# Convolution taps, channel statistics and the third branch's strips of a hybrid decoder layer in another order

## What is computed

```python
h = rms_norm(x) @ w_in                      # pool | u | v | a | g | gates 3*1024
p, u, v, ca, cg, gl = jnp.split(h, ...)
ya = pool_branch(p)                         # trailing-window means minus token, 4 linear maps
yb = u * (tril(W_s) @ layer_norm(v) + b)    # chunks of 128
y  = depthwise_conv31(ca * sigmoid(cg)) + conv_b
yc = silu(layer_norm(y))                    # mean and variance over 512 channels
ga, gb, gc = jnp.split(jax.nn.sigmoid(gl), 3, axis=-1)
merged = ga * (ya @ wb_pool) + gb * (yb @ wb_sgu) + gc * (yc @ wb_conv)
x = x + merged @ w_out
x = x + moe(rms_norm(x))                    # top 2 of 32 experts, 6.3 MB of weights each
```

## Time and profile before

| what | value |
|---|---|
| median of 3 runs | 1028.43 us (1027.98 to 1028.86) |
| the profiled execution | 1027.61 us, of which 1025.8 us are the span on the page |
| TensorE busy | 849.6 us (83%) |
| VectorE busy | 349.4 us (34%) |
| ScalarE busy | 199.2 us (19%) |
| mean granted clock of TensorE | 0.947 |
| bytes moved | 262.18 MB |

### The profile page before, as it was taken

How to read it: one execution, slowest core, us unless ns; L and a number is a source line. 1 busy time by engine, 2 the same in 40 slices (tenths; PEclk the granted TensorE clock), 3 DMA queues, 4 the chain that set the end, 5 groups by cost and what they waited for, 6 DMA issues and landing times.

```text
span 1025.8 us, 12405 instructions
## 1 busy us (share of the span) xinstructions
PE 849.6 (83%) x5199; PEld 582.1 (57%) x5199; DVE 349.4 (34%) x502; ACT 199.2 (19%) x304; POOL 89.3 (9%) x78
## 2 busy tenths in 40 slices
PE   1999999999999997996388898888878788787740
PEld 0899999999999997994133333323333223232310
DVE  3224856778777648125500000000000000000008
ACT  3421333222222353023011100100000001100003
POOL 2100000000000000000101111101101101011004
PEclk9999999999999998998599999999999989999995
DMA  9322222113133119737079999999999999999934
GB/s 276 107 83 83 83 83 81 42 50 128 62 107 121 42 54 357 292 124 292 17 282 420 420 420 419 419 418 420 419 418 420 421 419 421 420 419 419 412 137 194
DMA packets 73031, 262.18 MB, mean 256 GB/s; under 512 B 8359, under 2 KB 42307, under 8 KB 47840
## 3 DMA queue, kind: packets, MB, share of 16 engines
q1 hardware_dynamic: 67856, 252.46, 62.4%
q0 software_dynamic: 5120, 8.93, 2.4%
HBM read 256.09 MB, written 13.74 MB: 263 GB/s over the span
## 4 chain that ended last, share of the span: by engine, by line
PE 77%; DVE 11%; issue 6%; ACT 4%; DMA 2%; DVEq 0%; POOLq 0%; SPq 0%; ACTq 0%
PE ps L629 25%; PE ps L799 23%; PE ps L820 12%; PE ps L652 8%; PE ps L789 2%; PE ps L810 2%; DVE area L1438 2%; ACT area L1034 1%; DVE area L1113 1%; DVE xrows L1080 1%; ACT w_high L854 1%; DVE w_low L1100 1%; PE ps L600 1%; PE ps L714 1%; DVE xrows L1461 1%
## 5 line engine op out<-in xcount | busy, mean ns | idle before, releaser
L799 PE MATMUL ps<-area 128*64 128x512 f32 x1024 | 236.2, 615 | 29.8 <-issue 29.0
L799 PEld LDWEIGHTS ps<-area 128*64 128x64 f32 x1024 | 82.1, 141 | 181.5 <-issue 180.2
L629 PE MATMUL ps<-x_high,w_high 128*128 128x272 f32 x640 | 174.2, 290 | 0.6 <-DVE y_low L1258 0.6
L629 PE MATMUL ps<-x_low,w_high 128*128 128x272 f32 x640 | 173.3, 290 | 0.0
L1429 DVE TENSOR_TENSOR area<-ps,norm_cols 128x512 f32<-128x512 f32 x32 | 22.1, 692 | 432.3 <-PE ps L789 432.3
L820 PE MATMUL ps<-area 128*64 128x512 f32 x512 | 126.9, 641 | 14.8 <-ACT area L1034 14.8
L629 PE MATMUL ps<-x_high,w_low 128*128 128x272 f32 x640 | 133.1, 289 | 0.0
L629 PEld LDWEIGHTS ps<-x_high,w_high 128*128 128x128 f32 x640 | 121.1, 189 | 1.2 <-DVE w_low L1100 1.0
L629 PEld LDWEIGHTS ps<-x_low,w_high 128*128 128x128 f32 x640 | 121.2, 189 | 0.1
L1100 DVE TENSOR_TENSOR w_low<-area,w_high 128x2048 fp32r<-128x2048 f32 (+1 forms) x36 | 69.7, 1936 | 109.5 <-ACT w_high L854 109.5
L629 PEld LDWEIGHTS ps<-x_high,w_low 128*128 128x128 f32 x640 | 100.6, 189 | 0.0
(11 more groups left out here) (229 smaller groups left out, 860.1 us busy)
## 6 DMA issues: line engine op xcount, KB each, us to landing
area<-in_w_gate_e SPq DMA_DIRECT2D x32, 2048.0 KB, 32.4
area<-in_w_up_e SPq DMA_DIRECT2D x32, 2048.0 KB, 34.1
area<-in_w_down_e SPq DMA_DIRECT2D x32, 2048.0 KB, 34.4
area<-in_w_in SPq DMA_DIRECT2D x22, 1024.0 KB, 5.1
area<-in_w_out SPq DMA_DIRECT2D x4, 1024.0 KB, 10.5
area<-expert_rows SPq DMA_DIRECT2D x4, 1024.0 KB, 9.7
xrows<-in_x_prompt SPq DMA_DIRECT2D x4, 512.0 KB, 4.9
area<-in_w_branch_pool SPq DMA_DIRECT2D x4, 512.0 KB, 3.3
```

Of the source, the lines that this page charges most:

```text
L629: last = pe.matmul(ps[:, 2 * r + half, 0:HT], w[:, k, c * P:(c + 1) * P], src[:, k, half * HT:(half + 1) * HT], start=(k == 0 and len(part ...
L799: last = pe.matmul(ps[g * CAP:(g + 1) * CAP, 2 + s].rearrange("p (m f) -> p m f", m=2), xgT[s][:, k % 4, (k // 4) * CAP:(k // 4 + 1) * CAP ...
```

## The change

Four things are done. (1) The 124 taps are dealt out anew: the counts between VectorE's other steps differ, among them 8 in place of 4 between the variance of v and its reciprocal, and 13 in place of 12 ahead of `y_low[0]`; the last tap now stands in the second quarter of the second branch. (2) `mean` stands between the gate strip and the product strip of the second branch's third quarter, `var` in the same place of the fourth. (3) The third branch's strips go g0 b0 g1 b1 g2 g3 b2 b3 in place of g0 g1 g2 g3 b0 b1 b2 b3. (4) In the first 128 rows of `w_out` the terms of the low part for k below 6 come ahead of k = 6 and 7.

```diff
-    pairs += [in_pair(5 * W + 2 * D, j) for j in range(NJ)]
-    BC = len(pairs)
-    pairs += [branch_pair(2, j) for j in range(NJ)]
+    C_ORDER = [("g", 0), ("b", 0), ("g", 1), ("b", 1), ("g", 2), ("g", 3), ("b", 2), ("b", 3)]
+    pairs += [in_pair(5 * W + 2 * D, j) if name == "g" else branch_pair(2, j) for name, j in C_ORDER]
...
-                terms.sort(key=lambda t: t[1] is low)
+                terms.sort(key=lambda t: (t[0] >= KD - 2, t[1] is low))
...
+        for j in range(NJ):
+            column_pair(GB + 2 * j, xs, "gB", 2 * j)
+            if j == 2:
+                pe.wait_ge(tap_step, KW * TAPS)
+                pe.wait_ge(steps_done, KW)
+                channel_sum("mean", yc)
+            if j == 3:
+                pe.wait_ge(squared, KW)
+                channel_sum("var", squares)
+            column_pair(GB + 2 * j + 1, (y_high[1], y_low[1]), "bB", 2 * j)
+        for n, (name, j) in enumerate(C_ORDER):
+            if name == "g":
+                column_pair(GC + n, xs, "gC", 2 * j)
+            else:
+                column_pair(GC + n, (y_high[2], y_low[2]), "bC", 2 * j, (lambda k: (conv_low, k + 1)) if j == 0 else None)
...
+            if j == 2:
+                for q in range(KW):
+                    act.wait_ge(*((centred, q + 1) if q < KW - 1 else taken("mean")))
+                    s_.activation(squares[:, q], yc[:, q], ACT.Square).then_inc(squared, 1)
+            if j == 3:
+                act.wait_ge(*taken("var"))
+                s_.activation(row_a[:], row_a[:], ACT.Sqrt).then_inc(root, 1)
             act.wait_ge(product, pair_end(GB + 2 * j + 1))
             high(GB + 2 * j + 3)
...
+            if name == "g":
+                take_gates("gC", 2 * j)
+                high(GC + n + 2)
+            else:
+                act.wait_ge(product, done(f"bC{2 * j + 1}"))
+                high(GC + n + 2)
+                for i in (2 * j, 2 * j + 1):
+                    act.wait_ge(gate_spent, KD + i + 1)
+                    s_.copy(m_high[:, i], merged[:, i]).then_inc(merged_high, 1)
...
+        taps(16)
+        low(6)
         taps(8)
-        low(6)
-        taps(5)
...
-        taps(4)
+        taps(8)
         dve.wait_ge(root, 2)
...
+        taps(4)
         low(9)
...
+        pool_branch(0)
         times_u(0)
-        pool_branch(0)
+        taps(4)
         low(10)
...
+        taps(4)
         low(11)
...
+        taps(8)
         low(12)
...
-        taps(12)
+        taps(13)
         low(14)
...
-        taps(8)
+        taps(10)
         low(15)
...
-            taps(4 if j < NJ - 1 else 12)
+            taps(4 if j < NJ - 1 else 11)
```

More of the change, by code:

```diff
@@ L408, in program @@
     for j in range(NJ):
-        place_next(f"gB{2 * j}", f"gB{2 * j + 1}", f"bB{2 * j}", f"bB{2 * j + 1}")
-    place_next("gC0", "gC1", "gC2", "gC3", "mean", "gC4", "gC5", "var", "gC6", "gC7")
-    place_next(*[f"bC{i}" for i in range(8)])
+        place_next(f"gB{2 * j}", f"gB{2 * j + 1}")
+        if j == 2:
+            place_next("mean")
+        if j == 3:
+            place_next("var")
+        place_next(f"bB{2 * j}", f"bB{2 * j + 1}")
+    for name, j in C_ORDER:
+        place_next(f"{name}C{2 * j}", f"{name}C{2 * j + 1}")
     FIRST_ROWS = len(placed)
@@ L448, in pair_end @@
             return done(f"{'gb'[(n - GB) % 2]}B{(n - GB) // 2 * 2 + 1}")
-        if n < BC:
-            return done(f"gC{2 * (n - GC) + 1}")
-        return done(f"bC{2 * (n - BC) + 1}")
+        name, j = C_ORDER[n - GC]
+        return done(f"{name}C{2 * j + 1}")
     logit_halves = [(slice(0, NG + NE), slice(0, 2 * P)), (slice(CAP, CAP + NG + NE), slice(2 * P, T))]
@@ L705, in _ @@
         pe.wait_ge(sgu_low, KW)
-        for j in range(NJ):
-            column_pair(GB + 2 * j, xs, "gB", 2 * j)
-            column_pair(GB + 2 * j + 1, (y_high[1], y_low[1]), "bB", 2 * j)
         def channel_sum(name, src):
@@ L716, in channel_sum @@
             last.then_inc(product, 1)
[L718 to L726, removed]
-        for j in range(NJ):
-            column_pair(BC + j, (y_high[2], y_low[2]), "bC", 2 * j, (lambda k: (conv_low, k + 1)) if j == 0 else None)
+        for j in range(NJ):
+            column_pair(GB + 2 * j, xs, "gB", 2 * j)
[12 more added lines that the diff above has]
+                column_pair(GC + n, (y_high[2], y_low[2]), "bC", 2 * j, (lambda k: (conv_low, k + 1)) if j == 0 else None)
         for i in range(2):
@@ L967, in swish @@
         def swish():
-            act.wait_ge(*taken("var"))
-            s_.activation(row_a[:], row_a[:], ACT.Sqrt).then_inc(root, 1)
             for q in range(KW):
@@ L976, in swish @@
                 s_.copy(y_high[2][:, q], yc[:, q]).then_inc(conv_high, 1)
[L978 to L986, removed]
-        swish()
[L988 to L995, removed]
+        swish()
+        for n, (name, j) in enumerate(C_ORDER):
+            if name == "g":
[7 more added lines that the diff above has]
+                    s_.copy(m_high[:, i], merged[:, i]).then_inc(merged_high, 1)
         act.wait_ge(half_rows, 2)
@@ L1266, in _ @@
             merge_first(j)
-            taps(4 if j < NJ - 1 else 12)
+            taps(4 if j < NJ - 1 else 11)
         for j in range(NJ):
             low(20 + 2 * j)
-            taps(3)
+            if j == 2:
+                dve.wait_ge(product, done("mean"))
+                for q in range(KW):
+                    v.scalar_tensor_tensor(halves(yc[:, q]), of("mean"), -1.0 / W, halves(yc[:, q]), ALU.mult, ALU.add).then_inc(
+                        centred if q < KW - 1 else freed("mean"), 1)
+            if j == 3:
+                dve.wait_ge(product, done("var"))
+                v.tensor_scalar(halves(row_a[:]), of("var"), 1.0 / W, EPS, ALU.mult, ALU.add).then_inc(freed("var"), 1)
+                dve.wait_ge(root, 3)
+                own(v.reciprocal(row_a[:], row_a[:]))
+                for q in range(KW):
+                    v.tensor_tensor(yc[:, q], yc[:, q], row_a[:], ALU.mult).then_inc(scaled, 1)
+            if j < 2:
+                taps(6 if j == 0 else KW * TAPS - n_taps[0])
             low(21 + 2 * j)
             merge("B", j)
[L1273 to L1287, removed]
+            if j == 0:
+                taps(10)
         for q in range(KW):
@@ L1290, in _ @@
             v.tensor_tensor(y_low[2][:, q], yc[:, q], y_high[2][:, q].bitcast(F32), ALU.subtract).then_inc(conv_low, 1)
[L1291 to L1295, removed]
+        for n, (name, j) in enumerate(C_ORDER):
+            low(GC + n + 2)
+            if name == "b":
+                merge("C", j)
+                merged_low_part(j)
         dve.wait_ge(x_again, 32)
```

## The result

The changed kernel takes 1042.33 us (median of four executions, 1039.17 to 1043.62) where the kernel before takes 1028.24 us: a ratio of 1.0132, 95% interval 1.0108 to 1.0155, 14.1 us slower. Its profiled execution took 1043.62 us with a span of 1041.8 us, 16.0 more than the span before.

The account below looks back on a forecast made before the run. DMA was taken to bound the experts, TensorE the mixer, whose shifts reach the end one for one. 2.6 + 0.7 + 6.5 + 0.7 = 10.5 us on 1027.6, median 0.8 above: 1038.9 us; range 1034.5 to 1042.5.

Parts of the forecast that it names:

- rival E: Third branch: covers of 1.2 us at g1 and g2 fail, TensorE waits there too; 1041.9 us, chance 11%.
- Taps behind the variance: Before the chunk mixing: four more taps between variance of v and reciprocal lengthen TensorE's wait from 1.5 to 4.1 us, +2.6.
- The cover of the four taps behind `v_normed`: Four further taps ahead of a low part cost nothing, TensorE being at the chunk mixing; some tenths if uncovered.
- Taps ahead of `y_low[0]`: Pooling branch: one tap more ahead of `y_low` lengthens TensorE's wait of 0.6 us by 0.7 us.
- The tail: Before the rows of `w_out`: second strip lands 19.8 us after `gC7`, wait grows from 7.1 to 13.6 us, +6.5.
- Rival B: SyncE's queue at the mixer's end: quick landings, second strip in 17.1 us, tail grows by 3.7; 1036.1 us, chance 14%.
- C: Mixer's end: `w_out` loads stay hidden, tail wait stays 7.1 us, only the taps are paid; 1032.4 us, chance 5%.
- D: Mixer's end: cast of the first `w_out` strip starts early, removing wait and slow restart, 8.6 us; 1023.8 us, chance 3%.
- The clock: TensorE's granted clock behind the longer waits: 0.7 us taken for the chunk mixing's pause, 0 to 3.0 with the tail.

Follow-up runs that it names:

- the last kernel: Kernel before, last merge ahead of the low part not yet needed, no taps between variance of v and reciprocal, taps dealt out anew: 1018.36 us, ratio 0.9909.
- after_4taps: Changed kernel with four taps in place of eight between the variance of v and its reciprocal: 1034.31 us, ratio to before 1.0055.
- the last four experiments: Both suspected costs undone in the changed kernel, 1028.61 us; in the kernel before: six taps, 1030.87; last merge earlier, 1021.47; that plus taps dealt anew, 1018.36.

## Why the prediction was right, and where a term was off

- **Direction and bound.** The time went up, 1042.33 us against a forecast of 1038.9 with a range to 1042.5: 14.1 us where the sum had 10.5. That it stayed in the range, 0.2 us below its end, is in part luck: the forecast's own upper end was 1042.2 us, and the range reached further to hold most of rival E, which did not come. That the experts take over any shift one for one held: their stretch, routing and end included, differs by 0.5 us of 559.
- **Taps behind the variance.** Forecast +2.6 us and a wait of 4.1; measured 4.1. Reading the row of four taps in the chain, and doubling it, was enough. The cover of the four taps behind `v_normed` held: no wait came there.
- **Taps ahead of `y_low[0]`.** Forecast 1.3 us of wait; measured 1.2. What is waited for is the PSUM slot, as said above, and the forecast's words on it are off; its number does not depend on that.
- **The tail.** Forecast 13.6 us; measured 13.6, and the second strip landed 19.8 us after the first issue, as worked out from the landings of before. Within that sum two parts were off and made up for each other, so that it came out to the tenth is luck: the first transfer landed after 7.7 us and not 9.1, the second expert's after 399.76 + 16.0 = 415.8, 6.3 us behind `w_out` and not 5.0. Rival B, the quick queue, is thereby refused: it had 17.1 us for the second strip, though for the first transfer its 7.1 us were nearer to the 7.7 than the forecast's 9.1. The formula of the Trainium skill ("DMA: Bandwidth & Descriptors", section "Anatomy of one DMA — SWDGE (gpsimd) path") does not fit this queue either: the estimate by it was 16.4 us for the same bytes where 19.8 were measured. (With 16.4 us the sum comes to 1035.4 us, where the prediction has 1035.6.) The page states it for transfers of GpSimd's, and this queue is SyncE's.
- **Covers.** Rivals C, D and E did not come: both casts did wait for their loads, none started early, and no wait appeared at g1 and g2, whose cover was 1.2 us.
- **The clock: the term that was mis-sized.** It stood in the sum with 0.7 us and with 3.0 as its end. Measured in the profiled execution: 4.6 us in the chunk mixing, some 0.9 in the strip behind it, 0.6 more than before in the rows, about 6 in all. The step that failed took the restart behind the 7.1 us wait, 15 slow products with 1.5 us lost, as the most that a restart can cost. There the clock was back after 3.3 us. Here the pause stands ahead of the chunk mixing, and in this execution the clock stayed down to the end of the mixing and into the strip behind it, so the mixing's 5.8 us were nearly doubled. What decides how long the clock stays down is open: with the same pause the mixing took 10.3, 9.7 and 7.3 us in the profiled executions of three kernels. The Trainium skill ("TensorE: Matmul & The Clock Gate", section "HAM oscillation — how this bites in real kernels") has it that the work behind a long enough pause starts at half clock, and the trace agrees with a granted clock of 0.50 from 144.0 to 154.4 us. The price that the forecast took for such a restart, at most 1.5 us, came from another place in the kernel.
- **The rest** of the 14.1 us adds up: 7.2 us for the taps alone and 6.5 for the loads alone, both in the old kernel, make 13.7, the taps' clock included, and with both undone 0.6 us are left, which the interval does not tell from nothing.

## What to carry to other kernels

Work put into an engine's idle time is free only as far as that idle time reaches. Between the variance and its reciprocal VectorE had 0.27 us to spare; four more taps there cost their own 2.65 us, and in the changed kernel's profiled execution twice that again in TensorE's clock. When a wait in a DMA queue is tied to an instruction, moving that instruction moves every load queued behind it: look what those loads stand ahead of. And read the longest wait as an order: here the release that TensorE needed stood behind a step that nobody needed for another 14 us, and changing places was worth 6.5 us, where the new dealing out of the taps in the last kernel brought 3.1 by the medians.

## What the runs showed of the hardware

A pause of 1.5 us ahead of the chunk mixing left the granted clock at 1.00 (139 to 147 us) in the profiled executions of all five kernels that have it. With a pause of 2.8 us in one kernel and of 4.1 us in three it fell to 0.50, within the pause or just behind it. How long it stayed down differed between executions: with 4.1 us the mixing took 10.3, 9.7 and 7.3 us. The pause is a likely source of the spread with eight taps (1030.55 to 1036.30 us, where the kernel before stays within 1027.08 to 1029.42 beside it). It is not the only source: `after_4taps`, with 1.5 us, spreads as widely, and beside the last four experiments the kernel before itself goes from 1024.34 to 1029.73 us. At the end of the columns a pause of 1.8 us went with a fall of the clock in one kernel (0.87 from 400 to 405 us) and with full clock in another (1.00); what tells the two apart stays open.
